# Moving stages by slots in two timetables, and writing the convolution's phase tiles from VectorE

## The chip, the core and the metric

The kernel runs on one core of one Trainium2 chip. The metric is the device time of one execution in microseconds; the kernel before takes 786.01 us (median of 3 runs, 785.67 to 786.71). TensorE, VectorE, ScalarE, GpSimd and SyncE (here the DMA queue's issuer) run their own lists of instructions in order and wait for each other by semaphores.

## The reference, cut to what matters

Two transformer blocks over 256 tokens of width 1024, all in float32. The parts around the change:

```python
# first block: four mixers over one projection h @ w_in, per head of width 64
o_a = stick_breaking(qa, ka, va)         # 4 heads
o_b = dilated(qb, kb, vb)                # 4 heads, 3 windows each
o_c = forgetting(qc, kc, vc, cum)        # 4 heads
o_d = differential(qd, kd, vd, lam)      # 4 heads; then rms_norm over each head, * 0.8
branch = einsum('bsnc,ncd->bsnd', ys, w_branch)
x = x + sum(sigmoid(gate_logit) * branch) @ w_out
x = x + square(relu(rms_norm(x) @ w_up)) @ w_down

# second block: attention and a convolution over one projection
q, k, v, u = split(rms_norm(x) @ w_in)
q, k = apply_rope(rms_norm(q)), apply_rope(rms_norm(k))
a, g = split(u + glu_b)                  # 512 channels each
h = a * sigmoid(g)
h = causal_depthwise_conv(h, dw_w) + dw_b            # 31 taps
conv = silu(layer_norm(h))
x = x + concat([attn, conv]) @ w_out
x = x + (silu(h @ w_gate) * (h @ w_up)) @ w_down
```

## The kernel before, in words

All weight products run on TensorE in float32r with both factors split in a high and a low part, so that one product of 512 columns takes three matmuls (L607 to L609) for each of 4 chunks of 128 rows: 12 matmuls. A weight unit of 1 MB is loaded by SyncE into one of four `raw` buffers; ScalarE casts it to `whi` (`split_hi`, L1091) and VectorE subtracts to get `wlo` (`split_lo`, L1541). Both stand at fixed places between the products: ScalarE's `after(...)` comes at the head of a slot, before the slot's other stages, and VectorE's `before(...)` likewise.

**First block.** The projection has 18 chunks of 4 products: 72 slots. `timetable1()` says which small stages each engine runs in which slot; every engine goes through the same list of a slot in the same order, TensorE behind the slot's product. The attention tasks are numbered 0 to 7 (dilated), 8 to 15 (forgetting, "fox") and 16 to 23 (differential, "diff"), even numbers for the first 128 queries and odd ones for the second. A task that starts in slot a has its scores on TensorE in a (`z`), mask and maximum on VectorE and the exponentials on ScalarE in a + 1 (`x`), for diff tasks VectorE's combination of two maps in a + 2 (`cb`), the turn of the probabilities on TensorE in a + 3 (`t`), ScalarE's copy of it into `PT` in a + 4 (`pc`), the product with V on TensorE in a + 5 (`pv`) and VectorE's write into `ys` in a + 6 (`wr`). `Sb` and `PT` have two buffers each, used by even and odd tasks: VectorE's mask of task n (`z(n)` in VectorE's program, L1665) waits for the turn of task n - 2. `evac` empties a chunk's two PSUM banks on ScalarE in the last slot of a chunk and the first of the next. `tt` turns `ys`, `tu` splits the turned tile, `dn` and `de` norm the diff heads, with a power on GpSimd between them. `nl` prepares a fox head's forgetting terms on VectorE.

**Second block.** Its projection has 5 chunks, 20 slots, and `timetable2()`. `gt`/`gs` turn the gate half of u and take its sigmoid into `ca`; `ut` turns the other half into a PSUM bank and `ug` on VectorE (L1992) adds the bias and multiplies by the sigmoid. Channels 0 to 255 go to `ch` for VectorE's own convolution: 62 taps (`conv`, L2010), of which `cv` in the timetable runs 14 before the attention loop and the loop 48. Channels 256 to 511 went to `tg`, and ScalarE's `ph` copied them, even tokens into `hp` and odd ones into `odd`, from where a DMA brings them to the other half of the partitions of `hp`; TensorE convolves them (L923). For the four blocks of heads of q and k, `r0` squares and sums (ScalarE L1393, VectorE L1961), `ra` is the rope (L1980 to L1984), `r1` the last product (L1990), `r2` the turn on TensorE (L909) and ScalarE's copy into `qk2T`.

Of the kernel before, what the change touches and what calls it, by code (L numbers as in the profile page):

```python
# [94 lines left out]
def timetable1():  # L95

    bg = {s: [] for s in range(72)}
    for i, (c, col, dst, sc) in enumerate(QP):
        first = i == 0 or QP[i - 1][0] != c


        s = 4 * c + (4 if first else 6 if c == 6 else 5) if c < 8 else 43 if first else 45
        bg[s].append(("tp", i))
        bg[s + 1].append(("te", i))
    for h, a in enumerate((8, 9, 14, 15)):
        for k, name in ((0, "sz"), (1, "sm"), (2, "ss"), (4, "sc"), (5, "su"), (6, "sp"), (7, "so")):
            bg[a + k].append((name, h))
    starts = [24, 26, 28, 30, 32, 34, 36, 38]
    starts += [39, 40, 42, 43, 45, 46, 48, 49]
    starts += [51, 52, 54, 55, 57, 58, 60, 61]  # L110
    for n, a in enumerate(starts):
        kind, h, q = TASKS[n]
        if kind == "fox" and q == 0:
            bg[a - 1].append(("nl", h))
        if kind == "diff":
            stages = zip(range(7), ("z", "x", "cb", "t", "pc", "pv", "wr"))
        else:
            stages = zip((0, 1, 3, 4, 5, 6), ("z", "x", "t", "pc", "pv", "wr"))
        for k, name in stages:
            bg[a + k].append((name, n))  # L120
    bg[32].append(("fl", 0))
    bg[33].append(("fm", 0))
    bg[34].append(("fc", 0))
    bg[35].append(("fq", 0))
    for t in range(2):
        bg[56 + 3 * t].append(("tt", t))
        bg[57 + 3 * t].append(("tu", t))
        bg[68].append(("dn", t))
        bg[69].append(("de", t))
        bg[70].append(("tt", 2 + t))  # L130
        bg[71].append(("tu", 2 + t))
    rank = {"wr": 0, "so": 0, "fq": 0, "nl": 0}
    for s in bg:
        bg[s].sort(key=lambda x: rank.get(x[0], 1))
    return bg


def timetable2():


    bg = {s: [] for s in range(20)}
    bg[5] += [("gt", 0)]
    bg[6] += [("gs", 0), ("gt", 1)]
    bg[7] += [("gs", 1)]
    bg[8] += [("ut", 0), ("ug", 0)]
    bg[9] += [("ut", 1), ("ug", 1), ("ph", 0)]
    bg[10] += [("ph", 1)]
    for i, (a, b, c) in enumerate(((11, 13, 14), (12, 14, 15), (15, 17, 18), (16, 18, 19))):
        bg[a] += [("r0", i), ("ra", i)]
        bg[b].append(("r1", i))  # L150
        bg[c].append(("r2", i))
    for s, n in ((10, 7), (14, 3), (16, 2), (18, 2)):
        bg[s].append(("cv", n))
    rank = {"r1": 0, "ug": 0, "r0": 1, "ra": 1}
    for s in bg:
        bg[s].sort(key=lambda x: rank.get(x[0], 2))
    return bg
# [20 lines left out]
def build(nc, ctx, x_d, w_in, w_br, w_out, w_up, w_dn, w_in2, w_out2, w_g2, w_u2, w_d2, par_d, par2_d, cst_d, tw_d, out_d):  # L178
# [65 lines left out]
    def sem(name):  # L244
        return ctx.enter_context(nc.semaphore(name))
# [16 lines left out]
    s_e, s_pc, s_fl, s_sig, s_up = sem("s_exp"), sem("s_pcopy"), sem("s_fln"), sem("s_sigmoid"), sem("s_relu2")  # L262
    s_gs, s_rq, s_q2, s_ae, s_ac = sem("s_glusig"), sem("s_rsq"), sem("s_qk2"), sem("s_a_exp"), sem("s_a_copy")
    s_tri, s_aw, s_ln, s_sg, s_u2 = sem("s_masks"), sem("s_a_write"), sem("s_lnsilu"), sem("s_silu"), sem("s_gateup")
    s_ph = sem("s_phases")
    s_act = sem("s_act_step")

    s_lo, s_xg, s_xl, s_var, s_lam = sem("s_wlo"), sem("s_xgain"), sem("s_xlo"), sem("s_var"), sem("s_lam")
# [14 lines left out]
    def pcol(name, i=0, n=1):  # L283
        o, w = PAR[name]
        return par[:, o + i:o + i + n]
# [222 lines left out]
    @block.sync  # L508
    def _(e):
        w = Gate(e)  # L510
        def load(i):
            v, kn, n = units[i]
            if i >= NRAW:
                w.wait_ge(s_hi, HALF[i - NRAW])
                w.wait_ge(s_lo, HALF[i - NRAW])
            dst = raw[:, i % NRAW, 0:kn * n].rearrange("p (k n) -> p k n", k=kn)
            e.dma_start(dst, v).then_inc(d_raw[i % NRAW], 16)

        def load_piece(i, k):
            v, kn, n = units[i]  # L520
            e.dma_start(raw[:, i, k * n:k * n + n], v[:, k, :]).then_inc(d_piece[4 * i + k], 16)

        e.dma_start(cst[:, 0:136], cst_d[:, 0:136]).then_inc(d_cst, 16)
        e.dma_start(xr[:, 0, 0:512], x_v[:, 0, 0:512]).then_inc(d_x00, 16)
        load_piece(0, 0)
        e.dma_start(xr[:, 0, 512:1024], x_v[:, 0, 512:1024]).then_inc(d_x01, 16)
        for k in range(1, 4):
            load_piece(0, k)
        e.dma_start(xr[:, 1, :], x_v[:, 1, :]).then_inc(d_x1, 16)
        for k in range(4):  # L530
            load_piece(1, k)
        e.dma_start(par[:], par_d).then_inc(d_par, 16)
        load(2)
        load(3)
        e.dma_start(cst[:, 136:N0], cst_d[:, 136:N0]).then_inc(d_cs1, 16)
        e.dma_start(cs1[:], cst_d[:, N0:N0 + N1]).then_inc(d_cs1, 16)
        at = unit_of["up", 1, 0, 0]
        for i in range(NRAW, nu):
            if i == at:
                w.wait_ge(s_mix, 4)  # L540
                w.wait_ge(s_pm, 8)
                w.wait_ge(s_xl, X["M", 1, 1] + 1)
                e.dma_start(par2[:], par2_d).then_inc(d_par2, 16)
            if i == unit_of["p2", 3, 0, 0]:

                w.wait_ge(s_mm, done("dn", 7, 1, 1))
                for q in range(3):
                    e.dma_start(tw[:, q, :], tw_d[:, 2048 * q:2048 * q + 2048]).then_inc(d_tw, 16)
            if i == unit_of["wo2", 0, 1, 0]:

                w.wait_ge(s_ph, 2)
                for k in range(2):
                    e.dma_start(hp[64:128, 2 * k, 0:143], odd[0:64, k, 0:143]).then_inc(d_hp, 16)
                    e.dma_start(hp[0:64, 2 * k + 1, 0:143], odd[64:128, k, 0:143]).then_inc(d_hp, 16)
            load(i)
        for k in range(4):
            t, n = k // 2, k % 2
            w.wait_ge(s_res, 12 + k + 1)
            e.dma_start(o_v[:, t, 512 * n:512 * n + 512], xr[:, t, 512 * n:512 * n + 512]).then_inc(d_out, 16)
        w.wait_ge(d_out, 64)  # L560
# [4 lines left out]
    def _(e):  # L565
# [346 lines left out]
        def conv(m):  # L912

            i = m // 4
            if m == 0:
                w.wait_ge(s_ph, 2)
                w.wait_ge(d_hp, 64)
                w.wait_ge(d_tw, 48)
                clear(7)
            if m == 12:  # L920
                w.wait_ge(d_tw3, 16)
            for j in range(4 * (m % 4), 4 * (m % 4) + 4):
                ins = e.matmul(bank[7][:, 128 * i:128 * i + 128], tw[:, i % 3, 128 * j:128 * j + 128],  # L923
                               hp[:, i, j:j + 128], start=j == 0, stop=j == NSH - 1)
            if m % 4 == 3:
                ins.then_inc(s_cp, 1)
                gone[7] = (s_cf, 1)
# [147 lines left out]
    def _(e):  # L1075
# [299 lines left out]
                                   ACT.Sigmoid, bias=pcol("glu_b", 4 + k))  # L1375
            ins.then_inc(s_gs, 1)

        def ph(t):

            w.wait_ge(s_ug, t + 1)  # L1380
            w.wait_ge(s_pad, 1)
            u0 = 15 + 64 * t
            for k in range(2):
                u = tg[:, t, 128 * k:128 * k + 128].rearrange("p (u r) -> p r u", r=2)
                for i, p in ((2 * k, 0), (2 * k + 1, 64)):
                    e.copy(hp[p:p + 64, i, u0:u0 + 64], u[p:p + 64, 0, :])
                ins = e.copy(odd[:, k, u0:u0 + 64], u[:, 1, :])
            ins.then_inc(s_ph, 1)

        def r0(i):  # L1390
            w.wait_ge(s_ev, 36 + 4 + i + 1)
            w.wait_ge(s_var, RS[f"q{i - 2}"] + 1 if i > 1 else 0)
# [34 lines left out]
        def stages2(s):  # L1427
            for name, i in BG2[s]:
                if name == "gs":
                    gs(i)  # L1430
                elif name == "ph":
                    ph(i)
                elif name == "r0":
                    r0(i)
                elif name == "r2":
                    r2(i)
# [90 lines left out]
    def _(e):  # L1527
# [464 lines left out]
        def ug(t):  # L1992
            w.wait_ge(s_ut, 2 + t + 1)
            w.wait_ge(s_gs, t + 1)
            w.wait_ge(s_pad, 1)
            src = bank[tbank["u", 0, t]]
            for k in range(2):
                e.scalar_tensor_tensor(
                    out=ch[:, k, 30 + 128 * t:158 + 128 * t], in0=src[:, 128 * k:128 * k + 128],
                    scalar=pcol("glu_b", k), in1=ca[:, k, 128 * t:128 * t + 128], op0=ALU.add, op1=ALU.mult)  # L2000
            for k in range(2, 4):
                ins = e.scalar_tensor_tensor(
                    out=tg[:, t, 128 * k - 256:128 * k - 128], in0=src[:, 128 * k:128 * k + 128],
                    scalar=pcol("glu_b", k), in1=ca[:, k, 128 * t:128 * t + 128], op0=ALU.add, op1=ALU.mult)
            ins.then_inc(s_ug, 1)

        n_tap = [0]
# [282 lines left out]
```

## Time and profile before

| | |
|---|---|
| median of 3 runs | 786.01 us (785.67 to 786.71) |
| the profiled execution | 786.71 us, span 784.7 us |
| TensorE matmuls, busy | 773.0 us (99%) |
| VectorE, busy | 541.7 us (69%) |
| ScalarE, busy | 411.1 us (52%) |
| GpSimd, busy | 47.5 us (6%) |
| granted TensorE clock | 1.000 |

The span is the time from the first to the last instruction; 2.0 us of the execution lie outside it. A matmul's row shows it from its start to its modelled end, and the next one starts before that end, so a busy TensorE isn't read by the lengths of its rows but by how far apart they start. "L752" is line 752 of the kernel.

### The profile page before, as it was taken

The numbers are of one execution on the slowest core, as the hardware profiler recorded it, in microseconds if no ns is written. First come the engines' busy times: TensorE is split into PE (matmuls) and PEld (weight loads), VectorE is DVE, ScalarE is ACT, GpSimd is POOL, SyncE is SP. The second block draws the span as 40 slices with busy tenths as digits, with TensorE's granted clock in tenths as the row PEclk, the third lists the DMA queues.
The fourth block names the chain that finished last, engine by engine and source line by source line (L and its number), as shares of the span: only waits on it lengthen the run. The fifth ranks groups of instructions, "written<-read, shape, count | busy, mean of one in ns | idle before, by whom it ended". The sixth has DMA issues, their size and how long they took to land.

```text
span 784.7 us, 9739 instructions
## 1 busy us (share of the span) xinstructions
PE 773.0 (99%) x3850; PEld 650.0 (83%) x3850; DVE 541.7 (69%) x775; ACT 411.1 (52%) x554; POOL 47.5 (6%) x38
## 2 busy tenths in 40 slices
PE   6999999999999999999999999999999999999998
PEld 5888899888888888888888887888988888888896
DVE  5555364666775878587887748699857558668573
ACT  6556454554565745645455455764555344353441
POOL 0100000000001410000000004132000000000000
PEclk9999999999999999999999999999999999999999
DMA  9943434344544455656555663945133665655351
GB/s 328 341 151 93 135 106 161 123 148 160 161 137 186 162 185 182 218 203 212 174 188 178 213 215 128 356 157 172 55 95 121 217 202 175 210 175 200 108 161 53
DMA packets 68508, 136.24 MB, mean 174 GB/s; under 512 B 2416, under 2 KB 7152, under 8 KB 67824
## 3 DMA queue, kind: packets, MB, share of 16 engines
q1 hardware_dynamic: 68320, 134.59, 51.5%
q10 hardware_dynamic: 144, 1.05, 0.4%
q8 instruction: 30, 0.49, 0.3%
q14 instruction: 14, 0.11, 0.0%
HBM read 134.43 MB, written 1.05 MB: 173 GB/s over the span
## 4 chain that ended last, share of the span: by engine, by line
PE 92%; DVE 5%; ACT 1%; issue 1%; DMA 0%; SPq 0%; DVEq 0%; ACTq 0%
PE b L607 21%; PE b L609 20%; PE b L608 20%; PE SS L607 4%; PE SS L609 4%; PE SS L608 4%; PE TT L576 3%; PE OO L607 2%; PE OO L609 2%; PE OO L608 2%; PE OO L923 1%; PE SS L695 1%; DVE ca L2021 1%; PE b L752 1%; DVE wlo L1541 1%; PE SS L717 1%
## 5 line engine op out<-in xcount | busy, mean ns | idle before, releaser
L1541 DVE TENSOR_TENSOR wlo<-raw,whi 128x2048 fp32r<-128x2048 f32 (+2 forms) x123 | 274.7, 2235 | 95.5 <-ACT whi L1091 95.0
L1091 ACT CAST whi<-raw 128x2048 fp32r<-128x2048 f32 (+2 forms) x123 | 227.4, 1850 | 136.6 <-PE b L609 94.6
L607 PE MATMUL b<-whi,Ahi 128*128 128x512 f32 (+2 forms) x552 | 216.9, 393 | 1.6 <-DVE Alo L1564 1.4
L609 PE MATMUL b<-whi,Alo 128*128 128x512 f32 (+2 forms) x552 | 209.9, 380 | 0.0
L608 PE MATMUL b<-wlo,Ahi 128*128 128x512 f32 (+2 forms) x552 | 209.2, 379 | 0.0
L607 PEld LDWEIGHTS b<-whi,Ahi 128*128 128x128 f32 x552 | 104.5, 189 | 20.5 <-DVE Alo L1564 2.2
L609 PEld LDWEIGHTS b<-whi,Alo 128*128 128x128 f32 x552 | 104.3, 189 | 20.2
L608 PEld LDWEIGHTS b<-wlo,Ahi 128*128 128x128 f32 x552 | 104.7, 190 | 17.8
L1895 DVE STREAM_TRANSPOSE hT<-ust 32x256 f32<-32x256 f32 x160 | 69.7, 435 | 2.2
L607 PE MATMUL b<-whi,Bhi 128*128 128x512 f32 x154 | 60.4, 392 | 0.0
L609 PE MATMUL b<-whi,Blo 128*128 128x512 f32 x154 | 60.0, 389 | 0.0
L608 PE MATMUL b<-wlo,Bhi 128*128 128x512 f32 x154 | 59.9, 389 | 0.0
L607 PE MATMUL SS<-whi,hhi 128*128 128x512 f32 x108 | 42.0, 389 | 0.0
L608 PE MATMUL SS<-wlo,hhi 128*128 128x512 f32 x108 | 42.0, 389 | 0.0
L609 PE MATMUL SS<-whi,hlo 128*128 128x512 f32 x108 | 42.0, 389 | 0.0
L2149 POOL TENSOR_TENSOR st<-st 128x2 f32<-128x2 f32 (+3 forms) x13 | 20.5, 1580 | 250.1 <-DVE st L1574 250.1
L609 PEld LDWEIGHTS b<-whi,Blo 128*128 128x128 f32 x154 | 28.9, 188 | 6.0
L608 PEld LDWEIGHTS b<-wlo,Bhi 128*128 128x128 f32 x154 | 28.9, 188 | 5.9
L607 PEld LDWEIGHTS b<-whi,Bhi 128*128 128x128 f32 x154 | 28.9, 188 | 5.8
L1200 ACT ACTIVATE Sb<-Sb,st 128x384 f32<-128x384 f32 (+3 forms) x16 | 9.9, 618 | 33.7 <-DVE st L1689 33.7
L2021 DVE SCALAR_TENSOR_TENSOR ca<-ch,par,ca 128x256 f32<-128x256 f32 x58 | 23.8, 476 | 0.0
L607 PEld LDWEIGHTS SS<-whi,hhi 128*128 128x128 f32 x108 | 20.3, 188 | 4.2
(282 smaller groups left out, 1050.8 us busy)
## 6 DMA issues: line engine op xcount, KB each, us to landing
raw<-in_w_in SPq DMA_DIRECT2D x40, 1024.0 KB, 5.1
raw<-in_w_up SPq DMA_DIRECT2D x16, 1024.0 KB, 5.3
raw<-in_w_dn SPq DMA_DIRECT2D x16, 1024.0 KB, 5.0
raw<-in_w_d SPq DMA_DIRECT2D x11, 1024.0 KB, 5.0
raw<-in_w_g SPq DMA_DIRECT2D x10, 1024.0 KB, 5.1
raw<-in_w_u SPq DMA_DIRECT2D x10, 1024.0 KB, 5.1
raw<-in_w_out SPq DMA_DIRECT2D x8, 1024.0 KB, 5.0
raw<-in_w_br SPq DMA_DIRECT2D x4, 1024.0 KB, 5.2
```

The source lines that it names most:

```text
L576: ins = e.transpose(dst[:, 128 * k:128 * k + 128], src[:, 128 * k:128 * k + 128], ident)
L607: e.matmul(dst, xh, H[:, kc, c0:ce], start=first and kc == krs[0], stop=False)
L608: e.matmul(dst, xh, L[:, kc, c0:ce], start=False, stop=False)
L609: ins = e.matmul(dst, xl, H[:, kc, c0:ce], start=False, stop=last and kc == krs[-1])
L695: ins = e.matmul(SS[:, m * g:m * g + m], q, qkA[:, (4, 6, 10)[g] + pr, 0:m], start=True, stop=True)
L717: ins = e.matmul(Z[:, m * c:m * c + m], qkB[:, 4 * pr + 2 * a + c, qs], qkA[:, 4 + pr, 0:m], start=True, stop=True)
L1091: e.copy(whi[:, s, 0:m], raw[:, r, 0:m]).then_inc(s_hi, 1)
L1200: ins = e.activation(P, P, ACT.Exp, bias=stat_m[i][:, 0:1], accum_out=stat_s[i][:, 0:1])
L1541: e.tensor_tensor(wlo[:, s, 0:m], raw[:, r, 0:m], whi[:, s, 0:m].bitcast(F32), ALU.subtract).then_inc(s_lo, 1)
L1895: ins = e.transpose(dst[32 * m:32 * m + 32, :, :, 32 * i:32 * i + 32], src[32 * i:32 * i + 32, :, :, 32 * m:32 * m + 32])
L2021: k_tap[k] = own(e.scalar_tensor_tensor(out=ca[:, k, :], in0=x, scalar=tap, in1=ca[:, k, :], op0=ALU.mult, op1=ALU.add))
L2149: e.tensor_tensor(r, v, mhalf[:, 0:n], ALU.pow).then_inc(s_rs, 1)
```

## The change

In `timetable1()` the fox tasks start one slot later, the diff tasks start in pairs, both turns of the first half of ys stand in slot 55, and the norm of the diff heads and what follows it come earlier. In `timetable2()` the stage `ph` is gone and two of VectorE's taps move from slot 16 to slot 12. `ug` now writes `hp` and `odd` itself, in six instructions on 64 elements each instead of two on 128; the DMA and TensorE's convolution wait for `ug`'s semaphore.

```diff
-    starts += [39, 40, 42, 43, 45, 46, 48, 49]
-    starts += [51, 52, 54, 55, 57, 58, 60, 61]
+    starts += [40, 41, 43, 44, 46, 47, 49, 50]
+    starts += [51, 51, 54, 54, 57, 57, 60, 60]
...
     for t in range(2):
-        bg[56 + 3 * t].append(("tt", t))
-        bg[57 + 3 * t].append(("tu", t))
-        bg[68].append(("dn", t))
-        bg[69].append(("de", t))
-        bg[70].append(("tt", 2 + t))
-        bg[71].append(("tu", 2 + t))
+        bg[55].append(("tt", t))
+        bg[56].append(("tu", t))
+        bg[67].append(("dn", t))
+        bg[68].append(("de", t))
+        bg[68].append(("tt", 2 + t))
+        bg[69].append(("tu", 2 + t))
...
-    bg[9] += [("ut", 1), ("ug", 1), ("ph", 0)]
-    bg[10] += [("ph", 1)]
+    bg[9] += [("ut", 1), ("ug", 1)]
...
-    for s, n in ((10, 7), (14, 3), (16, 2), (18, 2)):
+    for s, n in ((10, 7), (12, 2), (14, 3), (18, 2)):
         bg[s].append(("cv", n))
...
             if i == unit_of["wo2", 0, 1, 0]:
-                w.wait_ge(s_ph, 2)
+                w.wait_ge(s_pad, 1)
+                w.wait_ge(s_ug, 2)
...
-        def ph(t):
-            w.wait_ge(s_ug, t + 1)
-            w.wait_ge(s_pad, 1)
-            u0 = 15 + 64 * t
-            for k in range(2):
-                u = tg[:, t, 128 * k:128 * k + 128].rearrange("p (u r) -> p r u", r=2)
-                for i, p in ((2 * k, 0), (2 * k + 1, 64)):
-                    e.copy(hp[p:p + 64, i, u0:u0 + 64], u[p:p + 64, 0, :])
-                ins = e.copy(odd[:, k, u0:u0 + 64], u[:, 1, :])
-            ins.then_inc(s_ph, 1)
...
-            for k in range(2, 4):
-                ins = e.scalar_tensor_tensor(
-                    out=tg[:, t, 128 * k - 256:128 * k - 128], in0=src[:, 128 * k:128 * k + 128],
-                    scalar=pcol("glu_b", k), in1=ca[:, k, 128 * t:128 * t + 128], op0=ALU.add, op1=ALU.mult)
+            u0 = 15 + 64 * t
+            for k in range(2):
+                a = src[:, 256 + 128 * k:384 + 128 * k].rearrange("p (u r) -> p r u", r=2)
+                g = ca[:, 2 + k, 128 * t:128 * t + 128].rearrange("p (u r) -> p r u", r=2)
+                bias = pcol("glu_b", 2 + k)
+                for i, p in ((2 * k, 0), (2 * k + 1, 64)):
+                    e.scalar_tensor_tensor(
+                        out=hp[p:p + 64, i, u0:u0 + 64], in0=a[p:p + 64, 0, :], scalar=bias[p:p + 64, :],
+                        in1=g[p:p + 64, 0, :], op0=ALU.add, op1=ALU.mult)
+                ins = e.scalar_tensor_tensor(out=odd[:, k, u0:u0 + 64], in0=a[:, 1, :], scalar=bias, in1=g[:, 1, :],
+                                             op0=ALU.add, op1=ALU.mult)
             ins.then_inc(s_ug, 1)
```

## Rows read from the trace of the kernel before

**Rows 1.** The page: busy us, share of the span, instructions.

```profile
PE 773.0 (99%) x3850; PEld 650.0 (83%) x3850; DVE 541.7 (69%) x775; ACT 411.1 (52%) x554; POOL 47.5 (6%) x38
```

**Rows 2.** TensorE's waits: for whom, us in total, times, longest.

```profile
...
PE TT L576 <- DVE PT L1990: 0.6, 1, 0.6
...
PE SS L707 <- DVE Sb L1669: 0.2, 1, 0.2
```

**Rows 3.** Time line of TensorE, two stretches: start, us, what ran [idle before].

```profile
...
234.22 0.38 PE L576 MATMUL TT<-cst,Sb 128*128 128x128 f32 x2
234.36 0.48 PE L607 MATMUL b<-whi,Ahi 128*128 128x512 f32 x1
...
236.98 0.39 PE L609 MATMUL b<-whi,Alo 128*128 128x512 f32 x1
...
249.08 0.39 PE L608 MATMUL b<-wlo,Ahi 128*128 128x512 f32 x1
...
251.35 0.39 PE L609 MATMUL b<-whi,Alo 128*128 128x512 f32 x1
251.58 1.03 PE L576 MATMUL TT<-cst,ys 128*128 128x128 f32 x8
252.37 0.48 PE L607 MATMUL b<-whi,Ahi 128*128 128x512 f32 x1
```

**Rows 4.** Time line of all engines around slots 52 and 53.

```profile
...
190.87 1.89 ACT L1091 CAST whi<-raw 128x2048 fp32r<-128x2048 f32 x1
...
191.91 1.03 PE L717 MATMUL SS<-qkA,qkB 128*128 128x256 f32 x4
192.66 0.36 ACT L1208 COPY PT<-TT 128x256 f32<-128x256 f32 x1
192.98 0.75 DVE L1681 SCALAR_TENSOR_TENSOR Sb<-cs,SS 128x256 f32<-128x256 f32 x2 [1.17 <-PE SS L717]
193.76 0.69 DVE L1687 TENSOR_REDUCE st<-Sb 128x2 f32<-128x512 f32 x1
...
194.49 0.51 ACT L1197 ACTIVATE Sb<-Sb,st 128x256 f32<-128x256 f32 x1 [1.46 <-DVE st L1687]
...
195.40 0.18 ACT L1197 ACTIVATION_READ_ACCUMULATOR Sb<-Sb,st 128x1 f32 x1
...
```

**Rows 5.** Time line of TensorE: two turns of q and k.

```profile
...
524.33 0.60 PE L576 MATMUL TT<-cst,PT 128*128 128x128 f32 x4
...
536.93 0.66 PE L576 MATMUL TT<-cst,PT 128*128 128x128 f32 x4 [0.61 <-DVE PT L1990]
...
```

**Rows 6.** VectorE's groups by form: busy us, mean ns of one, idle before.

```profile
...
L1630 DVE TENSOR_SCALAR qkB<-TT 32x512 f32<-32x512 f32 x4 | 2.7, 686 | 0.0
...
L2002 DVE SCALAR_TENSOR_TENSOR tg<-TT,par,ca 128x128 f32<-128x128 f32 x4 | 1.2, 345 | 0.0
...
```

**Rows 7.** Time line of VectorE in the second block's projection.

```profile
...
508.23 0.60 DVE L2002 SCALAR_TENSOR_TENSOR tg<-TT,par,ca 128x128 f32<-128x128 f32 x2
...
512.76 2.06 DVE L2021 SCALAR_TENSOR_TENSOR ca<-ch,par,ca 128x256 f32<-128x256 f32 x5
515.04 0.69 DVE L1961 TENSOR_REDUCE st<-tg 128x8 f32<-128x512 f32 x1 [0.23 <-ACT tg L1393]
...
522.85 0.68 DVE L1990 TENSOR_TENSOR PT<-PT,st 128x512 f32<-128x512 f32 x1
...
526.26 1.27 DVE L2021 SCALAR_TENSOR_TENSOR ca<-ch,par,ca 128x256 f32<-128x256 f32 x3
527.58 0.69 DVE L1961 TENSOR_REDUCE st<-tg 128x8 f32<-128x512 f32 x1
...
535.40 0.87 DVE L2021 SCALAR_TENSOR_TENSOR ca<-ch,par,ca 128x256 f32<-128x256 f32 x2
536.19 0.68 DVE L1990 TENSOR_TENSOR PT<-PT,st 128x512 f32<-128x512 f32 x1
...
```

**Rows 8.** Time line of ScalarE: the copies of `ph`.

```profile
...
508.86 0.51 ACT L1386 COPY hp<-tg 64x64 f32<-64x64 f32 x2 [1.83 <-DVE tg L2002]
509.38 0.25 ACT L1387 COPY odd<-tg 128x64 f32<-128x64 f32 x1
509.54 0.50 ACT L1386 COPY hp<-tg 64x64 f32<-64x64 f32 x2
...
```

More of the change, by code:

```diff
@@ L264, in build @@
     s_tri, s_aw, s_ln, s_sg, s_u2 = sem("s_masks"), sem("s_a_write"), sem("s_lnsilu"), sem("s_silu"), sem("s_gateup")
-    s_ph = sem("s_phases")
     s_act = sem("s_act_step")
@@ L915, in conv @@
             if m == 0:
-                w.wait_ge(s_ph, 2)
+                w.wait_ge(s_pad, 1)
+                w.wait_ge(s_ug, 2)
                 w.wait_ge(d_hp, 64)
@@ L1430, in stages2 @@
                     gs(i)
-                elif name == "ph":
-                    ph(i)
                 elif name == "r0":
```

## The prediction

> **What bounds the kernel now.** I read the page's busy time first: TensorE's matmul row is at 99% of the span [rows 1]. Then TensorE's waits: after the start of the program they come to little, and only two of them lie in code that the diff touches, 0.6 us of turns that wait for the rope product at L1990 and 0.2 us of the first fox scores at L707 [rows 2]. So an edit gains only what it takes out of TensorE's queue, and loses whatever makes TensorE stand. Last I read the time lines of the three engines slot by slot (a slot is one weight product of 12 matmuls and the small work behind it), because the edits shift work by slots and by fractions of a microsecond.
>
> **How TensorE's time adds up.** The last matmuls of an unbroken run start 0.227 us apart, so 11 intervals take 2.50 us; behind a break the 12 starts of a product spread over 236.98 - 234.36 = 2.62 us [rows 3]. A break of 8 turns costs 252.37 - 251.58 = 0.79 us and one of 2 turns 0.14 us [rows 3]: 0.108 a turn, with 0.08 off per break. A break thus has a fixed price of 0.12 - 0.08 = about 0.05 us beside its instructions.
>
> **Part 1, timetable1.** Fox tasks move one slot later, diff tasks start in pairs (51, 51, 54, 54, ...), the turns of ys and the norm of the diff heads come earlier. TensorE's instructions stay the same.
> - Breaks. Going through the slots 36 to 71 by hand, 32 of them hold TensorE work before and 27 after. 5 x 0.05 = 0.25 us gained.
> - The first fox scores move from slot 39 to 40, behind the masking of the last dilated scores that they wait for. That wait, 0.2 us [rows 2], goes.
> - The pair at 51. VectorE's z(n) waits for the turn of task n-2 (two Sb buffers). Task 16 wrote its scores' mask in slot 52 behind turn 14 of slot 51, task 17 in slot 53 behind turn 15 of slot 52. Now both stand in slot 52, while turn 14 is TensorE's last work of slot 52 and turn 15 its last of slot 53. Call T the end of turn 15. Queued behind that wait, in order: VectorE masks and maximum of task 17, from 192.98 (0.04 behind its scores' end) to 194.45, so T + 1.51; ScalarE's exponentials from 194.49 to 195.58, so T + 2.64 [rows 4]. Next in ScalarE's list stands slot 53: first the weight split L1091, 1.89 us, and only then pc(14), the copy that pv(14) in TensorE's slot 54 needs. ScalarE starts each 0.1 early (192.66 against 190.87 + 1.89), so the split ends at T + 4.43 and a copy of one block, taken as 0.26 of the 0.36 us for two blocks, at T + 4.6 [rows 4]; TensorE follows 0.05 later, as the turn at 536.93 does behind L1990 [rows 5, 7], T + 4.65. Undisturbed, pv(14) would start at T + 2.61: the turns of 234.22 end 0.38 later at 234.60, and the last matmul of the next product starts at 236.98, the following work 0.23 behind it [rows 3]. Loss 2.0 us. cb(16), cb(17) on VectorE end at about T + 3.8 and are covered by this; were the split not in between, cb(17) would be the late one, at a loss of about 0.9 us.
> - The later pairs (54, 57, 60) find their turns done a slot before. Their chains of about 4.5 us from scores to exponentials, with a split and an evacuation behind them, end some 0.8 us or more before TensorE asks (the tightest is the evacuation for slot 60). The same holds for turn 9, whose bank now waits for VectorE's four copies of q and k (2.7 us, [rows 6]): it comes free about as TensorE arrives. I take 0 for these, 0 to 0.3 us as bounds.
> - dn, de and the last turns of ys come one and two slots earlier; de ends about 1 us before TensorE's turn in slot 68 and nothing late waits for what follows. 0.
> Part 1: 2.0 - 0.25 - 0.2 = +1.6 us.
>
> **Part 2, the gated inputs of the convolution.** ph, 12 ScalarE copies of 64 elements, goes; VectorE writes hp and odd itself, 12 instructions of 64 elements for 4 of 128. ScalarE's release gives nothing: its next work in slot 11, the evacuation in front of the square for L1961, waits for TensorE's product.
> - Price of one. A 128-wide one takes 0.345 us, but two together 0.60, so they start 0.255 apart [rows 6, 7]. Five 256-wide taps start about 0.397 apart [rows 7], so 64 elements are worth 0.07: a 64-wide one lasts 0.275 and could be followed after 0.19. The four L1630 on 32 partitions each, though, do not overlap at all: 4 x 0.686 = 2.7 us of busy time, where the four L2002 give 1.38 in sum and 1.2 busy [rows 6]. ScalarE shows the same and its limit: L1387 on 128 partitions is overlapped by the copy on the first 64 behind it (509.54 against 509.38 + 0.25), but two L1386, on partitions 0 and 64, fill 0.50 for 2 x 0.25 [rows 8]. I take it that a change of the starting partition is what forbids overlap. In each group of three (0, 64, 0) two of the instructions are followed only at their end + 0.01.
> - Six thus cost 4 x 0.29 + 2 x 0.19 = 1.54 us where two cost 0.51: +1.03 for each token half, +2.06 for both. Bounds: all overlap, +1.26; none do, +2.46.
> - By the Trainium skill, VectorE: DVE Perf Modes, section Two Vector instructions with no wait between them, an instruction is held until all earlier ones end when its input or output starts in another quadrant of 32 partitions than the last. That gives the same four of six; a rule by partition count would give the none-overlap sum. The trace agrees as far as L1630 goes.
> - Is it hidden? Both halves and the split between them run back to back with the seven taps behind them; VectorE's only slack is the 0.23 us before L1961 at 515.04, and it overlaps 0.08 [rows 7]. So L1961 starts 2.06 - 0.31 = 1.75 us later. From there to L1990 at 522.85 VectorE never stands.
> - The taps. Two move from slot 16 to 12, ahead of the first L1990: 0.79 us more. It starts at 522.85 + 1.75 + 0.79 = 525.39, lasts 0.68, and TensorE turns at 526.12 instead of 524.33 [rows 5, 7]: 1.79 us of standing where there was none.
> - At the third head block L1961 (527.58) follows VectorE's own queue: three taps end at 527.53, plus 1.75 + 0.79, less 0.08 overlap: 529.99, 2.41 later. The two taps in front of L1990 at 536.19 are gone, so it runs at 536.19 - 0.79 + 2.41 = 537.81 to 538.49, and TensorE turns at 538.54 instead of 536.93 [rows 5, 7].
> Part 2: +1.6 us. The loss is one delay, not the sum of both waits. The same number of taps and the same queues stand behind it, so nothing of it is given back. The splits that move with it are 1 us or more ahead of their products. The DMA of odd into hp waits for the same time within half a microsecond and is used 25 us later: 0.
>
> **Sum.** +1.6 + 1.6 = +3.2 us on the profiled execution's own 786.7 us (span 784.7 and 2.0 around it). This execution is the highest of the three; on the median of 786.0 it gives 789.2 us.
>
> **The rivals.**
> - Slot 54 does not wait (not slower). If ScalarE had pc(14) done before task 17's exponentials, or turn 15 were early enough, the 2.0 us go: 787.2 us, within 0.2% of before, which is about what a measurement here can tell (784.4 to 787.6). For it: later pairs have slack of this size. Against it: the order of the two lists is fixed, and the chain needs more than T + 2.61 even without the split. It decides from a chain 2.0 us shorter. 9%.
> - The writes are hidden and only the taps' move acts: the wait at L1990 shrinks from 0.6 us to nothing, 2.0 - 0.45 - 0.6 gives 787.0 us. Against it: the 0.23 us of slack. 4%.
> - All narrow instructions overlap: VectorE is 0.8 us less late, 788.4 us. For it: nothing but L2002. 11%.
> - PSUM read at every second word is slow: the 12 instructions read so, and no VectorE row does it in PSUM. At half rate each costs 0.07 more, 0.8 in all: 790.0 us. 13%. The Trainium skill, SBUF - State Buffer, section Door 1, gives PSUM lines of two fp32 values and says that such patterns slow matmuls; no run here shows it for VectorE.
> - The forecast, 789.2 us: 61%. The last 2%: something I have not seen makes it faster by over 0.2%; all waits and breaks touched are worth 1.1 us together, less than the 1.6 us needed.
>
> **Range and chances.** From 787.5 (between no wait and overlap) to 790.4 (slow PSUM reads with 0.3 us of the small hazards): it leaves out the first two rivals, 13%, and some at the top. Faster 2%, within 0.2% 12%, slower 86%.
>
> **What would show it.** TensorE's waits list pv (L752) released by ScalarE's copy for about 2 us near 199 us, a wait for L1990 of about 1.8 us near 526 and one of about 0.5 near 538; L707 is gone from it. VectorE's new lines take about 1.5 us a half instead of 0.5. The forecast is wrong if ScalarE's split stands behind pc(14), or if L1961 starts less than 1 us later against TensorE's slot.

## The result, and the profile after

The changed kernel takes 790.8 us (median of 5, 788.46 to 791.29) against 786.0 before (785.42 to 786.71): ratio 1.0057, interval 1.0043 to 1.0073, 4.8 us slower. Forecast were 789.2, with a range up to 790.4. Its seven recorded executions fall in two groups by the mean granted TensorE clock: two at 1.000 took 788.2 and 788.5 us, five at 0.998 took 790.5 to 791.3. The profiled execution is one of the first: 788.22 us, span 786.4.

TensorE's waits in it (for whom, us in total, times, longest); they answer to [rows 2]. Lines are those of the new file, L751 is L752 of before, L1976 is L1990.

```profile
PE TT L575 <- DVE PT L1976: 2.0, 2, 1.7
PE OO L751 <- ACT PT L1208: 2.0, 1, 2.0
PE b L953 <- ACT ys L1413: 0.5, 2, 0.3
```

The wait at L707 is gone, one of 2.0 us has come in slot 54, and that for the rope product has grown from 0.6 to 2.0 us. The time line of all engines around slots 53 and 54 (TensorE's product rows left out):

```profile
192.97 0.38 PE L575 MATMUL TT<-cst,Sb 128*128 128x128 f32 x2
193.46 0.75 DVE L1667 SCALAR_TENSOR_TENSOR Sb<-cs,SS 128x256 f32<-128x256 f32 x2 [2.05 <-PE TT L575]
194.24 0.69 DVE L1673 TENSOR_REDUCE st<-Sb 128x2 f32<-128x512 f32 x1
...
194.97 0.51 ACT L1197 ACTIVATE Sb<-Sb,st 128x256 f32<-128x256 f32 x1 [2.64 <-DVE st L1673]
...
195.97 1.88 ACT L1091 CAST whi<-raw 128x2048 fp32r<-128x2048 f32 x1
...
197.75 0.52 ACT L1208 COPY PT<-TT 128x128 f32<-128x128 f32 x2
...
198.06 0.43 PE L751 MATMUL OO<-V,PT 128*128 128x64 f32 x2 [1.96 <-ACT PT L1208]
```

This is the chain of [rows 4] in its new order. Turn 15 ends at 193.35 (T); the mask of task 17 waits for it, its exponentials follow, then the split, and only then the copy. TensorE starts at T + 4.71. VectorE in the second block (answers to [rows 7]), and TensorE's two late turns (answers to [rows 5]):

```profile
507.82 0.61 DVE L1984 SCALAR_TENSOR_TENSOR ch<-TT,par,ca 128x128 f32<-128x128 f32 x2 [5.24 <-PE TT L575]
508.35 0.57 DVE L1993 SCALAR_TENSOR_TENSOR hp<-TT,par,ca 64x64 f32<-64x64 f32 x2
508.94 0.28 DVE L1996 SCALAR_TENSOR_TENSOR odd<-TT,par,ca 128x64 f32<-128x64 f32 x1
509.14 0.57 DVE L1993 SCALAR_TENSOR_TENSOR hp<-TT,par,ca 64x64 f32<-64x64 f32 x2
509.72 0.28 DVE L1996 SCALAR_TENSOR_TENSOR odd<-TT,par,ca 128x64 f32<-128x64 f32 x1
509.92 2.28 DVE L1527 TENSOR_TENSOR wlo<-raw,whi 128x2048 fp32r<-128x2048 f32 x1
...
516.97 0.69 DVE L1947 TENSOR_REDUCE st<-tg 128x8 f32<-128x512 f32 x1
```

```profile
526.31 0.66 PE L575 MATMUL TT<-cst,PT 128*128 128x128 f32 x4 [1.70 <-DVE PT L1976]
...
538.71 0.66 PE L575 MATMUL TT<-cst,PT 128*128 128x128 f32 x4 [0.34 <-DVE PT L1976]
```

The six narrow writes start at 508.35 and the split behind them at 509.92: 1.57 us for what took 0.51.

To compare traces I cut TensorE's time at four points: its first dilated scores (L695 before), its first turn of gates (498 us), its first turn for the LayerNorm (L1014, 575 us) and its last matmul. The first point lies 1.9 us earlier in this trace than in that of before (91.3 against 93.3 us); so the spans differ by only 1.7 us. The reason stands at the start of the program. TensorE's matmuls of a product start 0.43 us apart there, as at 1.2 GHz, until 9.6 us in this trace and until 13.5 us in that of before, then 0.23 apart, as at 2.4 GHz; 3.9 us at half speed are 1.9 us of work. This trace and then that of before (the profile gives no granted clock for this stretch):

```profile
9.16 0.61 PE L607 MATMUL b<-wlo,Ahi 128*128 128x512 f32 x1
9.59 0.42 PE L608 MATMUL b<-whi,Alo 128*128 128x512 f32 x1
```

```profile
12.63 0.63 PE L608 MATMUL b<-wlo,Ahi 128*128 128x512 f32 x1
13.06 0.63 PE L609 MATMUL b<-whi,Alo 128*128 128x512 f32 x1
```

In the traces below this moment lies anywhere from 9.6 to 13.8 us, with and without the change, so it is left out of the comparison. In the table all lengths are in us, from the traces' start times, and the sum is that of the last three stretches, without what lies before the first scores. A stand is what a matmul starts late against its usual distance.

```
trace                   clock  first scores  to gates' turn  to LayerNorm  to the end   sum
before                  1.000      93.26         404.71          76.95       206.24   687.90
changed                 1.000      91.34         406.75          78.53       206.26   691.54
part 1 alone            0.998      92.27         408.39          76.86       206.27   691.52
part 2 alone            1.000      92.83         404.73          78.56       206.29   689.58
17 in slot 52           0.998      92.45         409.17          78.53       206.26   693.97
changed, once more      0.998      91.51         408.29          78.54       206.25   693.09
pc(14) first            1.000      91.76         406.75          78.58       206.27   691.60
writes grouped          1.000      92.41         404.72          78.15       206.25   689.12
taps back in 16         1.000      92.07         404.75          78.57       206.25   689.57
fox shift, taps in 18   1.000      93.05         404.30          76.63       206.25   687.18
both copies first       1.000      91.69         405.42          78.54       206.28   690.24
17 in 52, turns back    0.999      93.27         404.57          78.58       206.31   689.46
fox, five taps          1.000      91.72         404.21          75.60       206.29   686.10
five taps alone         1.000      92.05         404.75          76.37       206.25   687.38
```

At full clock the change costs 2.04 us in the first stretch and 1.58 in the second, 3.64 in all, where the sum said 3.2. About 0.2 us comes back outside the span: 1.8 us of an execution lie there in all kernels with part 2, 2.0 in all others. That left open why most executions take 2 us more than this one.

One execution each of "17 in 52, turns back" and "fox, five taps" ran at a mean clock of 0.56 and 0.66 (1301 and 1109 us); the ratios below leave it out, and the medians would be 786.9 and 784.0 us without it.

### The profile page after: what moved, and what is told of

It reads as the page before. It is cut to its first block, busy times and chain, and to the rows that moved or that the text cites. A ratio compares the mean times of both kernels' runs of the same rounds, so it can differ in the third digit from the quotient of the medians.

```text
span 786.4 us, 9733 instructions
## 1 busy us (share of the span) xinstructions
PE 772.4 (98%) x3850; PEld 648.8 (82%) x3850; DVE 543.2 (69%) x783; ACT 408.9 (52%) x542; POOL 49.3 (6%) x38
## 3 DMA queue, kind: packets, MB, share of 16 engines
q10 hardware_dynamic: 144, 1.05, 0.4%
HBM read 134.43 MB, written 1.05 MB: 172 GB/s over the span
## 4 chain that ended last, share of the span: by engine, by line
PE 89%; DVE 7%; ACT 2%; issue 1%; DMA 1%; SPq 0%; ACTq 0%; DVEq 0%
PE b L606 20%; PE b L608 19%; PE b L607 19%; PE SS L606 4%; PE SS L608 4%; PE SS L607 4%; PE TT L575 3%; PE OO L606 2%; PE OO L608 2%; PE OO L607 2%; DVE wlo L1527 2%; DVE ca L2014 1%; PE b L751 1%; PE OO L923 1%; PE SS L694 1%
## 5 line engine op out<-in xcount | busy, mean ns | idle before, releaser
L2142 POOL TENSOR_TENSOR st<-st 128x2 f32<-128x2 f32 (+3 forms) x13 | 22.4, 1725 | 247.0 <-DVE st L1560 247.0
```

The lines of the kernel that those rows point to most:

```text
L2142: e.tensor_tensor(r, v, mhalf[:, 0:n], ALU.pow).then_inc(s_rs, 1)
```

## The experiments

**Part 1 alone, part 2 alone, task 17 moved back, and the changed kernel again.** The first has only the new `timetable1()`, the second only the rest. The third is the changed kernel with one number edited:

```diff
-    starts += [51, 51, 54, 54, 57, 57, 60, 60]
+    starts += [51, 52, 54, 54, 57, 57, 60, 60]
```

> Only timetable1 of the change; the second block is as before. By the sum of the prediction +1.6 us (2.0 lost at pv of slot 54, 0.25 and 0.2 gained), and the changed kernel's trace shows +2.0 for this stretch (2.1 of standing at L752's place). Open is why the changed kernel's median is 1.6 us above the sum, with a mean granted clock of 0.998 in most of its runs. Theory A: the 2.1 us of standing in slot 54 lets TensorE's clock fall in some executions; then this kernel shows 0.998 too and +3.5 to +4.5 us in those runs, +2.0 in the others. Theory B: the 1.8 us of standing before the first rope turn does it; then this kernel is at 1.000 in all runs and +2.0 us. Theory C: both places do it, each in part of the runs.

Measured: 789.4 us against 785.9, ratio 1.0037 (1.0027 to 1.0048). Two of eight executions had a clock of 1.000 and took 787.15 us, six had 0.997 or 0.998 and took 789.0 to 790.0. For the clock this is theory A. The times are below what was expected: 1.25 us over before for 2.0 at full clock, 3.1 to 4.1 for 3.5 to 4.5 at the lower one. The profile caught one of the six. TensorE in it:

```profile
198.99 0.43 PE L752 MATMUL OO<-V,PT 128*128 128x64 f32 x2 [1.97 <-ACT PT L1208]
199.26 0.50 PE L576 MATMUL TT<-cst,Sb 128*128 128x128 f32 x3
199.60 2.52 PE L717 MATMUL SS<-qkA,qkB 128*128 128x128 f32 x8
201.56 0.99 PE L607 MATMUL b<-whi,Ahi 128*128 128x512 f32 x1
202.34 0.63 PE L608 MATMUL b<-wlo,Ahi 128*128 128x512 f32 x1
202.77 0.63 PE L609 MATMUL b<-whi,Alo 128*128 128x512 f32 x1
203.20 0.44 PE L607 MATMUL b<-whi,Ahi 128*128 128x512 f32 x1
203.47 0.40 PE L608 MATMUL b<-wlo,Ahi 128*128 128x512 f32 x1
```

and the busy time of its engines by stretch (us and count of instructions, then the granted clock, DMA share and GB/s):

```profile
192.00:196.00 4.00, 4.00 (x20) 3.23 (x20) 1.91 (x6) 0.99 (x5) 0.00 (x0) 1.00 0.00 0
196.00:199.80 3.80, 1.83 (x12) 1.34 (x11) 2.61 (x9) 3.80 (x8) 0.00 (x0) 1.00 0.00 0
199.80:203.20 3.40, 3.40 (x12) 2.75 (x11) 3.33 (x11) 1.95 (x3) 0.00 (x0) 0.51 0.24 46
203.20:207.00 3.80, 3.73 (x23) 3.12 (x22) 2.97 (x3) 1.06 (x6) 0.00 (x0) 0.99 0.62 234
```

Behind the stand the granted clock is 0.51, the lower level of 1.2 GHz but for an edge, for 3.4 us: the eight score matmuls take 2.52 us instead of 1.48 and the products' matmuls start 0.43 apart instead of 0.23. Then it is back at 2.4 GHz. The Trainium skill, TensorE: Matmul & The Clock Gate, Part 1, says that the clock is granted by how busy TensorE has been; the trace agrees in that the fall comes right behind the stand. What it costs is read below, from two traces of the changed kernel.

> Only the second block's part of the change (narrow writes from VectorE, ph gone, two taps moved to slot 12); timetable1 as before. Sum and trace say +1.6 to +1.7 us, with standing of 1.8 us at the first rope turn and 0.5 at the third. Theory A (clock falls at slot 54): clock 1.000 in all runs, +1.7 us. Theory B (it falls here): 0.998 in most runs and +3 to +4 us. Theory C: some runs of each kind.

Measured: 787.46 us, ratio 1.0017 (1.0008 to 1.0025), +1.6 us as the sum had it, and 1.000 in all eleven executions, although TensorE stands 1.85 us before the first rope turn. Theories B and C are out: the clock does not fall here.

> The changed kernel with diff task 17 back in slot 52 (starts 51, 52, 54, 54, 57, 57, 60, 60); everything else of the change stays. My theory of the 2.0 us: task 17's mask waits for turn 15 and the copy of task 14 stands behind it. Then the wait of pv for ScalarE's copy in slot 54 is gone and the kernel is 2.0 to 2.1 us faster than the changed one at equal clock, about 787.7 us. Rival: pairs cost by themselves (bunched work on VectorE and ScalarE); then a wait of 1 us or more remains in slots 54 to 57. Theory A of the clock: 1.000 in all runs; theory B: 0.998 in most.

Measured: 791.77 us, ratio 1.007 (1.0058 to 1.0082): slower than the changed kernel. My edit had its own flaw. The wait of pv is gone, but the second turn of ys, which the change puts in slot 55, uses the PSUM bank of turn 17, and with task 17 in slot 52 its copy stands in slot 56. TensorE and ScalarE there:

```profile
205.38 0.35 ACT L1208 COPY PT<-TT 128x256 f32<-128x256 f32 x1
...
205.78 0.66 PE L575 MATMUL TT<-cst,ys 128*128 128x128 f32 x4 [3.16 <-ACT PT L1208]
```

Expected were 787.7 us. So this run says nothing on the pair itself, but one more thing on the clock: it is 0.996 to 0.998 in four of five executions, and in the traced one it fell right behind these 3.2 us of waiting.

> The changed kernel once more, beside the others on one chip and for a trace of an execution with the lower clock. Expected 790 to 791 us, +4 to +5 us, mostly at 0.998. If the profile falls on such an execution, the stretch at half clock lies behind slot 54 (theory A: 199 to 203 us) or behind the first rope turn (theory B: 526 to 530 us).

Measured: 790.45 us, ratio 1.0053 (1.004 to 1.0065); four of six at 0.998. From pv(14) to the second turn of ys its traced execution takes 205.56 - 198.19 = 7.37 us, and the full-clock trace 203.81 - 198.06 = 5.75: the fall costs 1.62 us. It lies at 198.5 to 201.9, where theory A had it.

**The split or the pair.** The changed kernel; in slot 53 ScalarE's stages stand in front of its split.

```diff
-                after("p1", c, ui, t)
...
-                stages1(4 * c + q)
+                early = 4 * c + q == 53
+                if early:
+                    stages1(53)
+                after("p1", c, ui, t)
...
+                if not early:
+                    stages1(4 * c + q)
```

> The changed kernel, with ScalarE's stages of slot 53 (the copy pc(14)) in front of its weight split. My chain: the copy then ends at T + 2.8 (T the end of turn 15), pv(14) waits 0.2 us, and VectorE's combination of task 17 is the late one: TensorE stands about 0.9 us in slot 54 in all instead of 2.1. With the shorter stand the clock should hold at 1.000; by both, 787.5 to 788 us, 2.5 to 3 us under the changed kernel's median. Rival (the split is not what makes it late, the pair is): still 2 us of standing and a clock of 0.998 in most runs.

Measured: 791.21 us, ratio 1.0071 (1.0057 to 1.0085), 0.998 in four of five, where 787.5 to 788 and a full clock were expected. The profile caught the fifth, at 1.000. pv(14) starts only 0.3 us late now (PEld is the load of its weights, with the wait), but two matmuls on, the turn of task 17 waits:

```profile
196.40 0.24 ACT L1208 COPY PT<-TT 128x128 f32<-128x128 f32 x1
196.55 1.90 ACT L1091 CAST whi<-raw 128x2048 fp32r<-128x2048 f32 x1
196.69 0.30 PEld L751 LDWEIGHTS OO<-V,PT 128*128 128x128 f32 x2 [0.56 <-ACT PT L1208]
196.70 0.43 PE L751 MATMUL OO<-V,PT 128*128 128x64 f32 x2
...
198.35 0.37 ACT L1208 COPY PT<-TT 128x256 f32<-128x256 f32 x1
...
198.86 0.41 PE L575 MATMUL TT<-cst,Sb 128*128 128x128 f32 x2 [1.61 <-ACT PT L1208]
```

Its PSUM bank is cleared by pc(15), behind the same split. Together they are as late as the one wait was: the first stretch is 406.75 us in both traces. The prediction said that without the split in between about 0.9 us would be left; that can hold only if both copies are out of its way. So:

```diff
+                s = 4 * c + q
+                if s != 53:
+                    if s != 54:
+                        after("p1", c, ui, t)
...
+                stages1(s)
+                if s == 54:
+                    after("p1", 13, 0, 1)
+                    after("p1", 13, 1, 0)
```

> The changed kernel with ScalarE's split of slot 53 behind both copies, pc(14) and pc(15), instead of in front of them. With only pc(14) in front, TensorE stood just as long, at the turn of task 17, whose PSUM bank waits for pc(15) behind the same split. Theory: the split's 1.9 us behind the late exponentials is what makes the stand; with both copies in front of it, what is late is VectorE's combination of task 17, and TensorE stands 0.9 to 1.0 us in slot 54 instead of 2.1. At that length the clock holds: 1.000 in most runs, time 2.8 to 3.2 us under the changed kernel, 787.5 to 788. Rival: the stand stays at 2 us, at a place further on in the slot. Rival on the clock: it falls whatever the length of the stand (the pair's small matmuls do it): 0.998 in most runs, 789.5.

Measured: 787.46 us, ratio 1.0026 (1.0016 to 1.0036), 1.000 in all nine. In the trace pv(14) is late by 0.30 us and turn 17, now behind VectorE's combination (L1692), by 0.44, 0.74 in all where 0.9 to 1.0 were expected:

```profile
196.63 0.30 PEld L751 LDWEIGHTS OO<-V,PT 128*128 128x128 f32 x2 [0.56 <-ACT PT L1208]
196.63 0.43 PE L751 MATMUL OO<-V,PT 128*128 128x64 f32 x2
...
197.46 0.44 PE L575 MATMUL TT<-cst,Sb 128*128 128x128 f32 x2 [0.28 <-DVE Sb L1692]
```

Moving two copies, 0.5 us together, in front of one split gives the changed kernel 3 us back: 1.3 of standing (406.75 to 405.42 in the table) and the fall of the clock.

**The pair undone with its neighbours.** As the third kernel above, with the turns and splits of ys back in their old slots:

```diff
-    starts += [51, 51, 54, 54, 57, 57, 60, 60]
+    starts += [51, 52, 54, 54, 57, 57, 60, 60]
...
-        bg[55].append(("tt", t))
-        bg[56].append(("tu", t))
+        bg[56 + 3 * t].append(("tt", t))
+        bg[57 + 3 * t].append(("tu", t))
```

> The changed kernel with task 17 in slot 52 and the turns of ys back in slots 56 and 59 (splits 57 and 60), which the kernel with only the first of these edits lacked: there the second turn of ys waited 3.2 us for pc(17). Theory: no stand over 0.3 us is left in slots 51 to 57, clock 1.000, and the time is part 2's 1.6 us less 0.4 to 0.5: 787.0 to 787.2. Rival (pairs at 54, 57 and 60 cost too): a stand of 0.5 us or more in slots 56 to 60 and 787.7 or more.

Measured: 787.15 us, ratio 1.0015 (1.0006 to 1.0024); the clock is 0.999 or 1.000 in the other ten. The largest stand in slots 51 to 60 is 0.21 us, behind a turn of ys. The pairs at 54, 57 and 60 are harmless; the first one, whose buffers the fox tasks still hold, and the turns of ys moved up behind it are the whole loss of part 1: without them the first stretch is 404.57 us, 0.14 less than before.

**What makes narrow writes dear.** Part 2 alone with the six instructions of `ug` in another order:

```diff
-            for k in range(2):
-                ... hp[0:64], hp[64:128], odd
+            for half in range(2):
+                for k in range(2):
+                    if half == 0:
+                        ... odd
+                    ... hp[64 * half:64 * half + 64]
```

> Part 2 alone, its six narrow instructions in another order: the four that start at partition 0 first, the two that start at partition 64 last. Theory: an instruction is followed at its end only where the starting partition changes, twice instead of four times a half: 1.34 us for six instead of 1.54, 0.4 us less on VectorE for both halves, TensorE's stand before the first rope turn 1.45 instead of 1.85 us. Rival: fewer than 128 partitions forbid overlap, which are four of six in either order: no change. Third: it depends on the width alone, no change either. In time 0 to -0.4 us against part 2 alone (787.5).

Measured: 786.76 us, ratio 1.0014 (1.0006 to 1.0023). VectorE's rows (the instructions on partitions 0 to 63, 0 to 63 and twice 64 to 127 at the end):

```profile
507.39 0.28 DVE L1995 SCALAR_TENSOR_TENSOR odd<-TT,par,ca 128x64 f32<-128x64 f32 x1
507.58 0.27 DVE L1997 SCALAR_TENSOR_TENSOR hp<-TT,par,ca 64x64 f32<-64x64 f32 x1
507.77 0.27 DVE L1995 SCALAR_TENSOR_TENSOR odd<-TT,par,ca 128x64 f32<-128x64 f32 x1
507.96 0.78 DVE L1997 SCALAR_TENSOR_TENSOR hp<-TT,par,ca 64x64 f32<-64x64 f32 x3
508.77 2.29 DVE L1527 TENSOR_TENSOR wlo<-raw,whi 128x2048 fp32r<-128x2048 f32 x1
```

A write on 64 partitions from 0 is followed after 0.19 us when the next one starts at partition 0 too; in the changed kernel the same write was followed after 0.28, by one that starts at 64. Six take 1.38 instead of 1.57 us, the stand before the first rope turn is 1.48 instead of 1.85 us, and the stretch up to the LayerNorm is 0.41 us shorter (78.15 for 78.56). The two kernels' ratios (1.0014 and 1.0017) don't resolve that much; the traces do. The count of partitions doesn't matter, the change of start does; input and output change together here, so which of them counts is not told apart.

**Where the taps stand.** Part 2 alone, `cv` as ((10, 7), (14, 3), (16, 2), (18, 2)).

> Part 2 alone with its two taps back in slot 16 (10: 7, 14: 3, 16: 2, 18: 2). Theory: VectorE's queue has no slack between the writes and the third rope product, so the taps' place only moves the stand: about 1.1 us before the first turn and 1.3 us before the third, the same end, +1.6 us against before. Rival: the taps in slot 12 cost by themselves, and this kernel is 0.5 to 0.8 us faster than part 2 alone.

Measured: 787.03 us, ratio 1.0017 (1.0008 to 1.0026). Stands of 1.05 and 1.28 us before the first and the third rope turn, and 78.57 us in the table for 78.56. Shifting the taps neither cost nor gained.

**Towards a faster kernel.** From the kernel before, with `ph` on ScalarE: first the fox shift alone and `cv` as ((10, 7), (14, 3), (18, 4)).

> The kernel before with two edits: the fox tasks one slot later (diff tasks, turns and norm as before) and the two taps of slot 16 moved to slot 18 (10: 7, 14: 3, 18: 4); ph stays on ScalarE. The wait at L707 (0.3 us) goes, no stand in slot 54. The stand of 0.8 us at the third rope turn goes as well. Theory V: VectorE's queue bounds the stretch up to the end of the attention loop, so TensorE gives these 0.8 us back in the loop and the kernel is 0.3 us faster than before. Rival: the stand is gained: 1.0 us faster (784.9).

Measured: 785.11 us against 785.86, ratio 0.999 (0.9982 to 0.9999). The stands at L707 and before the third rope turn are gone, but the one before L953 near the end of the attention loop has grown from 0.47 to 0.96 us: 0.3 + 0.8 gained and 0.5 given back, between the two theories. If the loop's end was waiting for VectorE, fewer taps in the loop take that stand out:

```diff
-            conv(6 if k < 8 else 1)
+            conv(5 if k < 8 else 4)
```

> The kernel before with the fox shift and 14 taps as 7, 3 and 4 in slots 10, 14 and 18, and, new, five taps instead of six in each of the eight turns of the attention loop, the missing eight behind it (4 and 4). Theory V (VectorE's queue bounds the stretch up to the end of the loop and has slack behind it): the stand of 1.0 us before L953 goes, 0.8 to 1.3 us faster than the same without this edit, 783.8 to 784.3. Rival: the last taps are then late for the LayerNorm's turns (L1014) and 0 to 1 us is lost there.

> The kernel before with only the loop's taps changed, five per turn and eight behind the loop. Theory V: of the stands at L953 (0.5 and 0.35 us) the first goes, 0.5 us faster than before at most; the wait for L1990 (0.6 us) stays. Rival: nothing changes, since those waits are ScalarE's.

Measured, with the shift: 784.12 us, ratio 0.998 (0.9971 to 0.9989), against both kernels the fastest. Alone: 785.16 us, ratio 0.9993 (0.9984 to 1.0002), which the timing can't tell from no change; its trace is 0.5 us shorter. Both came out as expected. Of the two stands before L953 at the end of the loop (0.47 and 0.35 us before) the first is gone in both, the second is left, and nothing is late at L1014. So the first was VectorE's. The loop's last rows of the faster kernel:

```profile
562.81 0.33 PE L953 MATMUL b<-V,PT 128*128 128x64 f32 x2
...
565.01 0.41 PE L953 MATMUL b<-V,PT 128*128 128x64 f32 x2 [0.19 <-ACT ys L1425]
```

## Why the prediction was wrong in size and right in its steps

- **Slot 54 (2.0 us): the step that failed.** It was right in its place, its releaser and its length: 2.12 us, T + 4.71 for T + 4.65. What failed is that the sum took a stand of 2.0 us to cost 2.0 us and put nothing for TensorE's clock; no rival named it either. In most executions the clock falls behind the stand, and that costs 1.6 us more in the trace (7.37 against 5.75 us). The term was mis-sized: 2.1 + 1.6 = 3.7 us where the clock falls. The kernel with both copies first, in which neither the long stand nor the fall is left, is 3 us faster.
- **How the rest adds up.** With the 1.6 us the sum of 3.2 is 4.8, the measured difference, but that it fits to the tenth is luck. The traces' own difference with the fall is 693.09 - 687.90 = 5.2 us, 5.0 with the 0.2 us outside the span, and the start of the program varies by more than what is left. It is luck too that the two executions at 1.000 (788.2 and 788.5 us) lie within the range: the traced one costs 3.64 us behind the first scores, over the 3.2 of the sum, and reached them 1.9 us early.
- **Later pairs, 0 to 0.3 us.** Taken at 0, it was 0.30: in slot 55 the second turn of ys waits for pc(17), and this one for pv(15) of the same slot, because PT too has two buffers. I had followed the PSUM banks but not PT.
- **Breaks, -0.25 us.** Overrated. With 2.12 and 0.30 of stands and 0.32 gained at the fox scores, 2.04 in all leaves 0.06 us for five breaks fewer.
- **The first fox scores, -0.2 us.** Right; 0.32 by start times.
- **Part 2, +1.6 us.** Right: 1.58 us in the trace, 1.6 by the runs of part 2 alone. 1.57 for 1.54 us a half, 1.86 for 1.79 us at the first turn, 538.71 against 536.93, less the 0.12 us by which 498.09 lies behind 497.97, gives 1.66 for 1.61 at the third. The second stretch leaves no room for a gain by ScalarE's release.
- **Narrow instructions.** The rival that all overlap and the one that PSUM read at every second word is slow are out: six writes take 1.57 us for 1.14 if all overlap, and a 128-partition write of 64 elements takes 0.285 us, 0.01 over the 0.275 estimated from contiguous ones, and is followed after 0.19 to 0.20 for the 0.19 estimated. The order of the writes confirmed the change of start as the cause.
- **The rivals of the other side** are out: slot 54 waits, and the writes were not hidden.

Open: the timed executions at full clock are 2.4 us faster than the others, the traces explain 1.6 of it. In both traces that kept the full clock behind such a stand TensorE had come to 2.4 GHz early in the program (at 9.6 and 10.6 us) and the first scores came early too (91.3 and 91.8 us); in the three in which it fell these are 10.7 to 12.1 and 91.5 to 92.5 us. So the rest may be that the executions which keep the clock are those that started early; five traces don't show it, and of the timed ones only the mean clock is on record.

## What to carry to other kernels

Before pairing two tasks, follow every double buffer of the pair (here Sb, PT and the PSUM banks) to the task that still holds it, and read what stands behind the waiting instruction in its engine's list: a 2 us split behind a late exponential is what made this wait long. A stand of an otherwise full TensorE is not always worth its length alone: the one of 2.1 us cost 3.7 in most executions, and two of 0.7 us together only themselves. Where VectorE's queue had no slack, two taps moved from slot 12 to 16 moved the stand and not the end; eight moved behind the loop gained 0.6 us there (76.95 to 76.37).

## What the runs showed of the hardware that I had not expected

- TensorE's mean clock was 0.997 or 0.998 in 19 of 26 executions of three kernels that are late by 2.1 us in slot 54 (two of seven and two of six of the changed kernel, two of eight of part 1 alone and one of five with pc(14) first kept it). Two traces show the place: 1.2 GHz for 3.4 us behind the stand. Behind 1.85 us of standing before the first rope turn it kept 1.000 in all eleven executions of part 2 alone, and behind 0.74 us in slot 54 in all nine with both copies first. The length of one stand doesn't tell them apart: with pc(14) first the lateness in slot 54 is 0.30 and 1.78 us, neither of them as long as 1.85, and yet the mean clock was 0.998 in four of five (none of these was traced); the sum of both, 2.1 us, still could. Before the rope turn TensorE had run products without a break for 13.5 us; before slot 54 it had gone through small work in every slot. That this makes the difference is not shown.
- On VectorE, a 64-element instruction on 64 partitions is followed after 0.19 to 0.21 us or after 0.28, by whether the next one starts at the same partition.
